# An encoder's RWKV-7 recurrence: each chunk's triangular inverse built as a matrix of its own from powers in 64x64 tiles

## The reference

```python
def _rwkv7_step(S, inp):
    r, w, k, v, a, b = inp
    Sa = jnp.einsum('zbhvk,zbhk->zbhv', S, a)
    S = S * w[..., None, :] + Sa[..., :, None] * b[..., None, :] + v[..., :, None] * k[..., None, :]
    return S, jnp.einsum('zbhvk,zbhk->zbhv', S, r)
```

## Time and profile before

| | |
|---|---|
| time, median of 3 runs | 2095.07 us (2093.65 to 2096.19) |
| profiled execution, its own time | 2095.07 us |
| its span | 2093.1 us |
| TensorE busy | 1840.8 us (88%) |
| VectorE busy | 484.6 us (23%) |
| ScalarE busy | 400.9 us (19%) |
| GpSimd busy | 53.5 us (3%) |
| recurrence, eight pairs | 439.3 to 802.4 us |

### The profile page before, as it was taken

One profiled execution on the slowest core, in us unless ns is written; L12 is line 12 of the kernel. 1 busy time (PEld: TensorE's weight loads), 2 busy tenths in 40 slices (PEclk: granted clock), 3 DMA queues, 4 the chain that ended last, 5 costly groups with the idle time before them and its releaser, 6 DMA issues.

```text
span 2093.1 us, 29565 instructions
## 1 busy us (share of the span) xinstructions
PE 1840.8 (88%) x11998; PEld 1345.0 (64%) x11998; DVE 484.6 (23%) x1116; ACT 400.9 (19%) x1077; POOL 53.5 (3%) x94
## 2 busy tenths in 40 slices
PE   4999999879999999999959988888888998888882
PEld 3788888568889995466647555555645556555451
DVE  1111100677777763010240000000000000000003
ACT  2310000555556551011210000000000000000001
POOL 0000000000000000000000000000000000000000
PEclk9999999979999999999969999999999999999996
DMA  8424653000000007354226999999999999999993
GB/s 286 161 81 161 113 131 141 1 1 1 0 0 0 0 1 274 135 194 161 86 81 256 428 432 418 420 425 434 423 428 420 431 419 425 429 435 428 430 419 159
DMA packets 93162, 505.82 MB, mean 242 GB/s; under 512 B 39076, under 2 KB 43416, under 8 KB 74680
## 3 DMA queue, kind: packets, MB, share of 16 engines
q1 hardware_dynamic: 85456, 487.62, 57.6%
q0 software_dynamic: 6656, 14.12, 1.9%
q10 hardware_dynamic: 1000, 3.37, 0.5%
HBM read 498.76 MB, written 18.91 MB: 247 GB/s over the span
## 4 chain that ended last, share of the span: by engine, by line
PE 69%; DMA 21%; DVE 4%; ACT 3%; issue 2%; SPq 1%; DVEq 0%; ACTq 0%; POOLq 0%
DMA ring<-in_wu 18%; PE ps L1558 16%; PE ps L1211 13%; PE ps L1455 5%; PE ps L1597 5%; PE ps L1548 5%; PE ps L1372 3%; PE ps L1391 3%; PE ps L1473 3%; DMA ring<-in_wd 2%; PE ps L1347 2%; PE ps L1397 1%; PE ps L1514 1%; PE ps L1482 1%; SPq L264 1%
## 5 line engine op out<-in xcount | busy, mean ns | idle before, releaser
L1558 PE MATMUL ps<-ring,rkv 128*64 128x256 f32 x4096 | 484.9, 399 | 73.9 <-DMA ring<-in_wu 42.9
L1558 PEld LDWEIGHTS ps<-ring,rkv 128*64 128x64 f32 x4096 | 335.6, 144 | 232.4 <-DMA ring<-in_wu 51.2
L1211 PE MATMUL ps<-hnT,ring 128*128 128x256 f32 (+1 forms) x1280 | 280.7, 382 | 6.4 <-ACT gg L455 2.2
L1211 PEld LDWEIGHTS ps<-hnT,ring 128*128 128x128 f32 (+1 forms) x1280 | 240.3, 188 | 47.1 <-issue 8.7
L1597 PE MATMUL ps<-ring,gg 128*64 128x512 f32 x1024 | 231.9, 606 | 23.1 <-DMA ring<-in_wd 11.9
L1597 PEld LDWEIGHTS ps<-ring,gg 128*64 128x64 f32 x1024 | 82.3, 139 | 150.6 <-issue 136.6
L1157 DVE SCALAR_TENSOR_TENSOR gg<-ps,tmp,gg 128x256 f32<-128x256 f32 x32 | 15.5, 484 | 532.0 <-PE ps L1558 532.0
L1548 PE MATMUL ps<-hnT,sw 128*128 (+1 forms) x1024 | 120.8, 280 | 7.4 <-DVE hnT L1141 7.4
L1548 PEld LDWEIGHTS ps<-hnT,sw 128*128 128x128 f32 x1024 | 117.8, 195 | 13.3 <-issue 13.3
L1372 PE MATMUL ps<-ring 128*128 128x128 f32 x768 | 114.7, 276 | 0.1
L1372 PEld LDWEIGHTS ps<-ring 128*128 128x128 f32 x768 | 100.3, 192 | 0.8 <-ACT ring L545 0.3
(11 more groups left out here) (315 smaller groups left out, 1719.1 us busy)
## 6 DMA issues: line engine op xcount, KB each, us to landing
ring<-in_wg SPq DMA_DIRECT2D x32, 4096.0 KB, 19.9
ring<-in_wu SPq DMA_DIRECT2D x32, 4096.0 KB, 20.6
ring<-in_wd SPq DMA_DIRECT2D x32, 4096.0 KB, 18.0
ring<-in_w_in SPq DMA_DIRECT2D x7, 4096.0 KB, 14.3
ring<-in_w_out SPq DMA_DIRECT2D x4, 4096.0 KB, 15.8
ring<-in_w_in SPq DMA_DIRECT2D x16, 512.0 KB, 7.5
ring<-in_xatt_wk SPq DMA_DIRECT2D x1, 4096.0 KB, 13.6
ring<-in_xatt_wv SPq DMA_DIRECT2D x1, 4096.0 KB, 13.6
```

The lines of the kernel that those rows point to most:

```text
L1211: ins = mm(ps[0:rows_, t % 4, 0:T], lhs, hnT[:, k, :], start=k == 0, stop=k == KD - 1)
L1558: ins = mm(ps[CAP * h:CAP * h + CAP, bank, 0:T], xT[:, k, CAP * i:CAP * i + CAP], slot_k(slot)[:, k, T * h:T * h + T], start=k == 0, stop= ...
```

## The change

The inverse is no longer applied to X level by level. It is built as a matrix R of its own, and X is multiplied by it once, at the end.

- R begins as I + A, which GpSimd writes for each direction (two additions of 64 partitions x 256 columns each). At each level the square of the power and the power's product with R come out of one set of products, with the same weights, `PN`. GpSimd adds the product to R in levels 1 to 4; VectorE does the last addition, after level 5 (L1014 in the new numbering).
- The products use only the blocks on the diagonal: weights of 64x64 at partitions 0 to 63 and 64 to 127, the output in the same partitions. A group's four products at a level write 64 columns each in levels 0 and 5 and 128 in levels 1 to 4. All four write bank `2 * g`.
- The power and R lie packed in `PR`, 448 columns a group; ScalarE copies 192 (level 0) or 320 columns from PSUM. TensorE turns the power after each of levels 0 to 4 (five times; four before). The turned power is copied to `PN` by ScalarE for groups 0 and 2 and by VectorE for groups 1 and 3.
- The turned old keys (`BKh`) are made after the levels (four pairs of transposes, copied by ScalarE), where before they stood ahead of them.
- VectorE's loop has 10 steps, one for each of its copies to `PN`, and the elementwise work stands behind other steps. Moved to ScalarE: `keys`, and the scaling in `scaled_keys`. Moved to GpSimd: `before` (QA and Q1) and the product in `scaled_keys`.
- ScalarE's square roots stand after level 2, the first half of the exponentials after level 4 and ahead of the old keys, the second half after X's copy.
- TensorE's eight pairs are written out; there is no loop.

The tiles:

```diff
-        PT = W[:, 9216:10240].rearrange("p (g e n) -> p g e n", g=4, e=2)
-        PN = W[:, 10240:11264].rearrange("p (g e n) -> p g e n", g=4, e=2)
+        PR = W[:, 9216:11008].rearrange("p (g n) -> p g n", g=4)
+        R = PR[:, :, 5 * CH:7 * CH].rearrange("p g (e n) -> p g e n", e=2)
+        PN = W[:, 1024:2048].rearrange("p (g e n) -> p g e n", g=4, e=2)
...
+        def two_blocks(x, c, first, second):
+            return x[CH * c:CH * c + CH].rearrange("p (s n) -> p s n", n=CH)[:, first:second + 1:second - first, :]
...
```

GpSimd, in each pair:

```diff
+                    pool.wait_ge(S["rw_about"], p + 1)
+                    pool.tensor_tensor(ew[:, QA], ew[:, Q0], sw[:, 0, ds(p + 1, 1), :].rearrange("p o t -> p (o t)"), ALU.subtract)
+                    pool.tensor_tensor(ew[:, Q1], sw[:, 1, ds(p + 1, 1), :].rearrange("p o t -> p (o t)"), ew[:, CS1],
+                                       ALU.subtract).then_inc(S["rw_q"], 1)
+                for z in range(2):
+                    pool.wait_ge(S["rw_mask"], 4 * p + 2 * z + 2)
...
+                    for c in range(2):
+                        q = slice(CH * c, CH * c + CH)
+                        one = ident[q, q].unsqueeze(1).unsqueeze(1).broadcast_to([CH, 2, 2, CH])
+                        ins = pool.tensor_tensor(R[q, 2 * z:2 * z + 2], GB[q, 2 * z:2 * z + 2, :, 0, q], one, ALU.add)
+                    ins.then_inc(S["rw_r1"], 1)
+                for l in range(1, 5):
+                    for g in range(4):
...
+                        pool.wait_ge(S["rw_pte"], 20 * p + 4 * l + g + 1)
+                        pool.tensor_tensor(PR[:, g, 5 * CH:], PR[:, g, 5 * CH:], PR[:, g, 3 * CH:5 * CH], ALU.add).then_inc(S["rw_ra"], 1)
+                    if l == 2 and not last:
+                        scaled_keys(p)
...
```

ScalarE, in each pair:

```diff
                 for l in range(5):
+                    for g in range(4):
+                        powers(l, g)
+                    for g in (0, 2):
+                        turned_powers(l, g)
...
+                    if l == 2 and not first:
                         head_std(p - 1)
+                    if l == 2 and not last:
                         key_norm(p + 1)
+                if not last:
+                    exponentials(p + 1, 0)
+                for g in range(4):
+                    old_keys(g)
+                for g in range(4):
+                    act.wait_ge(S["rw_xx"], 4 * p + g + 1)
+                    A(X[:, g].rearrange("p m e n -> p (m e n)"), ps[:, 2 * g, 0:T], ACT.Copy).then_inc(S["rw_xe"], 1)
+                if not last:
+                    exponentials(p + 1, 1)
```

VectorE, in each pair:

```diff
-                for step in range(24):
-                    g = step % 4
-                    dve.wait_ge(S["rw_xm"], 24 * p + step + 1)
...
-                    V.tensor_tensor(xf, xf, ps[:, 2 * g, 0:T], ALU.add).then_inc(S["rw_xa"], 1)
+                for step in range(10):
+                    l, g = step // 2, 1 + 2 * (step % 2)
+                    dve.wait_ge(S["rw_tr"], 20 * p + 4 * l + g + 1)
...
+                    V.tensor_copy(PN[:, g].rearrange("p e n -> p (e n)"), ps[:, 2 * g + 1, T:2 * T]).then_inc(S["rw_pnv"], 1)
...
+                for g in range(4):
+                    dve.wait_ge(S["rw_xm"], 4 * p + g + 1)
+                    V.tensor_tensor(PR[:, g, 5 * CH:], PR[:, g, 5 * CH:], ps[:, 2 * g, 3 * CH:5 * CH], ALU.add).then_inc(S["rw_xa"], 1)
```

TensorE, the levels, the product of R and X, and the pairs:

```diff
                         for e in range(2):
-                            o = ps[:, 2 * g, 0:T].rearrange("p (m e n) -> p m e n", m=2, e=2)[:, :, e, :]
-                            ins = mm(o, power(e), X[:, g, :, e, :], start=True, stop=True)
...
-                            for e in range(2):
-                                ins = mm(ps[:, 2 * g + 1, P * e:P * e + P], PN[:, g, e, :], power(e), start=True, stop=True)
-                            ins.then_inc(S["rw_pt"], 1)
+                            for c in range(2):
+                                q = slice(CH * c, CH * c + CH)
+                                if l == 0:
+                                    o, rhs = ps[q, 2 * g, CH * (e + c):CH * (e + c) + CH], GB[q, g, e, 0, q]
+                                elif l < 5:
+                                    o, rhs = two_blocks(ps[:, 2 * g, :], c, e + c, 3 + e), two_blocks(PR[:, g, :], c, e + c, 5 + e)
+                                else:
+                                    o, rhs = ps[q, 2 * g, CH * (3 + e):CH * (4 + e)], R[q, g, e, :]
+                                ins = mm(o, PN[q, g, e, q], rhs, start=True, stop=True)
...
+                for g in range(4):
+                    pe.wait_ge(S["rw_x0ev"], 4 * p + g + 1)
+                    pe.wait_ge(S["rw_xa"], 4 * p + g + 1)
+                    for e in range(2):
+                        for c in range(2):
+                            q = slice(CH * c, CH * c + CH)
+                            o = ps[q, 2 * g, 0:T].rearrange("p (m e n) -> p m e n", m=2, e=2)[:, :, e, :]
+                            ins = mm(o, R[q, g, e, :], X[q, g, :, e, :], start=True, stop=True)
+                    ins.then_inc(S["rw_xx"], 1)
...
-            pair_(0, True, False)
-            with pe.Fori(0, CT - 2) as i:
-                pair_(i + 1, False, False)
-            pair_(CT - 1, False, True)
+            for p in range(CT):
+                pair_(p, p == 0, p == CT - 1)
```

More of the change, by code:

```diff
@@ new lines, in scaled_keys @@
+            def scaled_keys(p):
+                pool.wait_ge(S["rw_kd0"], p + 1)
+                for z in range(2):
+                    ins = pool.tensor_tensor(ew[:, KD0 + z], ew[:, KD0 + z],
+                                             rkv[:, ds(p + 9, 1), :].rearrange("p o t -> p (o t)"), ALU.mult)
+                ins.then_inc(S["rw_kd1"], 1)
+            with pool.Fori(0, CT - 1) as i:
+                pair_(i, False)
+            pair_(CT - 1, True)
+            pool.wait_ge(S["rw_xa"], 4 * CT)
@@ L551, in pair_ @@
-                    if l == 4 and not last:
-                        for half in range(2):
-                            exponentials(p + 1, half)
-                    if l < 4:
-                        for g in range(4):
-                            act.wait_ge(S["rw_tr"], 16 * p + 4 * l + g + 1)
-                            A(PN[:, g].rearrange("p e n -> p (e n)"), ps[:, 2 * g + 1, T:2 * T], ACT.Copy).then_inc(S["rw_pne"], 1)
-                    if l == 1 and not first:
+                        powers(l, g)
@@ L559, in pair_ @@
+                    for g in (0, 2):
+                        turned_powers(l, g)
+                    if l == 0 and not last:
+                        for z in range(2):
+                            ins = A(ew[:, KD0 + z], aa[:, z, ds(p + 1, 1), :].rearrange("p o t -> p (o t)"), ACT.Identity,
+                                    scale=prm[:, ds(p + (P_KA + 1), 1)], bias=dprm[:, ds(p + 31, 1)])
+                        ins.then_inc(S["rw_kd0"], 1)
+                    if l == 2 and not first:
                         head_std(p - 1)
-                    if l == 1 and not last:
+                    if l == 2 and not last:
@@ L905, in pair_ @@
                 if not last:
-                    keys(p + 1)
                     for z in range(2):
@@ L916, in pair_ @@
                         deviation(p - 1, free)
-                    if step == 4 and not first:
+                    if step == 1 and not last:
+                        square_sums(free)
+                    if step == 2 and not first:
                         variance(free)
-                    if step == 5 and not last:
-                        square_sums(free)
-                    if step == 20 and not last:
+                    if step == 9 and not last:
                         bonus(p + 1, free)
-                    xf = X[:, g].rearrange("p m e n -> p (m e n)")
@@ L954, in pair_ @@
+                if not last:
+                    products_bk(p + 1, 0)
                 for g in range(4):
@@ L1377, in pair_ @@
-                        if (l, g) == (1, 0) and not first:
-                            pe.wait_ge(S["rw_dsq"], p)
-                            ins = mm(free, ones2, DSQ, start=True, stop=True)
-                        if (l, g) == (1, 1) and not last:
-                            pe.wait_ge(S["rw_sq"], p + 2)
-                            ins = mm(free, ones2, ew[:, SQ], start=True, stop=True)
-                        if (l, g) == (5, 0) and not last:
-                            pe.wait_ge(S["rw_bonus_in"], p + 2)
-                            ins = mm(free, ones2, ew[:, BON], start=True, stop=True)
@@ L1386, in pair_ @@
[L1386 to L1393 removed]
+                            pe.wait_ge(S["rw_pnv"] if g % 2 else S["rw_pne"], 10 * p + 2 * (l - 1) + g // 2 + 1)
@@ L1394, in pair_ @@
+                        ins.then_inc(S["rw_pt"] if l < 5 else S["rw_xm"], 1)
+                    if l < 5:
                         for g in range(4):
                             pe.wait_ge(S["rw_pte"], 20 * p + 4 * l + g + 1)
+                            free = ps[:, 2 * g + 1, 0:T]
```

(12 more changed lines are left out.)

117 lines of the change are left out of this document (63 added, 54 removed).

## The result

| | before | after |
|---|---|---|
| median | 2094.36 us (2092.67 to 2096.19, 4 runs) | 2135.77 us (2134.42 to 2138.65, 4 runs) |
| profiled execution, its span | 2095.07, 2093.1 us | 2134.42, 2132.6 us |
| recurrence, first Gram product to the last pair's end | 439.27 to 802.41: 363.14 us | 438.10 to 841.04: 402.94 us |
| a middle pair | 45.06 to 45.43 us | 49.95 to 53.36 us |

The changed kernel is slower: ratio 1.0199, 95% interval 1.0182 to 1.0217. The forecast was 2115 us with a range to 2133: the side was right, the size half of what came, and the time lies above the range. All of it is in the recurrence (39.8 us longer in the trace; the span 39.5).

The account below looks back on a forecast made before the run. TensorE was taken to bound the recurrence (44.07 of 45.25 us busy a pair). Later start 4.0 less 0.55 won back gives 3.45 us a pair, +19.6 in all on 2095.07: 2115 us, 8-in-10 range 2088 to 2133.

Parts of the forecast that it names:

- level 1 starts: Level 1 waits for GpSimd's additions for R and starts at 11.7 us of the pair, against 12.46 before.
- wait in level 3, group 3: TensorE waits 2.65 us for VectorE's copy of group 3, behind table load, root and reciprocal.
- wait in level 5: TensorE waits 2.3 us for VectorE's last group 3 copy, behind `products_ar` waiting for exponentials; level ends at 33.4.
- counterpart of L1404 (L1484): Starts at 36.65 us of the pair against 32.67, after old keys' transposes and R times X: 4.0 us later.
- the walk: One steady pair followed step by step through TensorE and the engines it waits for: 3.45 us a pair slower.
- That rival's 2165: Diagonal tiles don't run side by side: groups cost 0.9 instead of 0.45, about +9 a pair, 2165 us; chance 0.08.
- 19.6: Slowdown of the whole kernel in us: six middle pairs 20.7, first pair about +0.5, last about -1.6.
- the switches of shape: TensorE's changes of tile shape, 14 in a pair before L1404's counterpart, cost 0.17 us each.
- the faster rival: Free shape switches (2.4 us a pair), cheaper GpSimd additions (level 1 up to 1.7 earlier): both 2084 us; chance 0.16.
- A lower clock is no case of its own: TensorE's clock stays at 1.00, as in 380 to 390, where it pauses in every step; no cost counted.
- About 0.28 apart: At the pair's end, spacing in us of ScalarE's eight copies of old keys, from 33.95 on, before X's first copy.
- 8.6 + 4 x 0.74 = 11.7 with hand-overs: GpSimd's start: after VectorE's 8.6 us, QA, Q1 and two additions at 0.74 each make R for direction 0.

Follow-up runs that it names:

- e9: The kernel before with TensorE's eight pairs written out, nothing else: 2094.81 us, ratio 1.0003.
- e2 to e4: The changed kernel with one move each: R's additions first on GpSimd; VectorE's waiting instructions behind group 3's copies; old keys early: 2109.28, 2112.20, 2122.10 us.
- e6: The changed kernel with logarithm and exponential on ScalarE in place of roots, reciprocals and their table loads: 2102.36 us, ratio 1.0039.
- e1: The changed kernel with 50 useless transposes a pair in TensorE's three long waits: 2124.03 us, ratio 1.0151.
- e7: The changed kernel with R first, keys early, logarithm and exponential for roots, VectorE's work reordered behind its copies: 2043.09 us, ratio 0.9760.
- e5: The changed kernel with R first on GpSimd, VectorE's waiting instructions behind group 3's copies and old keys early, all together: 2084.63 us, ratio 0.9955.

## Why the prediction was half right

Step by step, from the pair's first product (measured: the pair at full clock):

| step | forecast | measured |
|---|---|---|
| level 1 starts | 11.7 | 12.18 |
| level 2, level 3 start | 15.85, 18.9 | 16.24, 19.20 |
| wait in level 3, group 3 | 2.65 | 2.59 |
| level 4 starts; its waits | 24.6; 0.4 and 1.2 | 24.92; 0.28 and 0.85 |
| wait in level 5; its end | 2.3; 33.4 | 2.38; 33.9 |
| counterpart of L1404 (L1484) | 36.65 | 38.08 |
| its four groups | 3.15 | 3.15 |
| the rest of the pair | 8.9 | 8.72 |
| pair | 48.7 | 49.95 |

The rest is 0.2 us shorter because the loop is gone, as in e9.

**Right.** TensorE's products became too short to cover the other engines, and the waits came where the walk had them, on the engines that it named. The prices held: 0.45 us for a group of 64x64 tiles, 0.73 us for GpSimd's 256 columns, 0.27 instead of 0.30 for level 0. e2 to e4 and e6 show that each of these waits is a cause. The rivals fell. Tiles pair: sixteen products in 1.94 us, both tiles in one bank. By the Trainium skill ("TensorEngine Tiling (Array Packing)", Restrictions and Gotchas) different row tiles can't access the same PSUM bank at once; for diagonal tiles this trace shows otherwise. (That rival's 2165 was also too high by its own terms: 19.6 and, in eight pairs, half of 11 us give 2159.) And the switches of shape cost 0.12 us each instead of 0.17: level 2 lasts 2.96 us (659.33 to 662.29), 0.25 more than 1.8 + 0.91. That goes the faster rival's way, and is too little for it. TensorE's busy share of the recurrence was forecast at about 85%; it is 82%, with the low clock in it.

**Wrong, the larger part: "A lower clock is no case of its own".** It gave a reason, the attention window at clock 1.00 with TensorE pausing in every step. But TensorE was busy 8.93 of 10 us there, and its pauses were short ones:

```profile
384.34 0.66 PE L1299 MATMUL ps<-cst_sb,tmp 128*128 128x128 f32 x4 [0.34 <-ACT tmp L487]
...
387.04 0.66 PE L1299 MATMUL ps<-cst_sb,tmp 128*128 128x128 f32 x4 [0.20 <-ACT tmp L487]
```

The pauses that the forecast itself had worked out, 2.65 us in level 3 and 2.3 us in level 5, had no counterpart there, so the row could not clear them. The one ahead of level 1 the walk had at 0.8 us or more (11.7 - 10.9); it is 2.41 us. e1 puts the price at 11.6 us. With it the first pair is 2.8 us longer than before (forecast 0.5) and the last 1.0 us longer (forecast 1.6 shorter); without it, in e1, they are 1.3 longer and 1.45 shorter.

**Wrong, two terms mis-sized.** "About 0.28 apart" for the copies of old keys, from L557's four in 1.21 us: these copies, of 64 partitions each and in turn of one half and of the other, came 0.39 us apart (3.15 us for eight), 0.9 us a pair. And GpSimd's start: "8.6 + 4 x 0.74 = 11.7 with hand-overs" left 0.14 us for all hand-overs, and level 1 started 0.5 us later. QA began 0.26 us after VectorE's last signal, and Q1 (L365) took 0.91 instead of 0.73 us beside VectorE's L944, which had begun 0.15 us before it:

```profile
652.49 0.48 DVE L944 TENSOR_TENSOR tmp<-tmp 128x256 f32<-128x256 f32 x1
```

In the first pair, which has no such instruction of VectorE there, Q1 took 0.71 us. In e7 the same two meet with Q1 (L379) ahead, and VectorE's (L948) is the long one; alone, in the last pair, it takes 0.43 us:

```profile
564.96 0.73 POOL L379 TENSOR_TENSOR tokA<-sw,tokA 128x256 f32<-128x256 f32 x1
```

```profile
565.06 0.91 DVE L948 TENSOR_TENSOR tmp<-tmp 128x256 f32<-128x256 f32 x1
```

The Trainium skill says that GpSimd shares its SBUF interfaces with VectorE's instructions that have two SBUF inputs ("GPSIMD Engine Reference", section 1). The traces agree: one of the two pays, in these rows the one that starts second.

**The sum.** Forecast 19.6. At full clock (e1) the recurrence is 391.30 - 363.14 = 28.2 us longer: 4.7 us in each of six middle pairs instead of 3.45, and 0.9 us more than forecast in the first and last pair together. The clock adds 11.6: 39.8, as the trace has it. The medians are 41.4 apart; the profiled execution was the fastest of its four.

## What to carry to other kernels

When a change shortens the bounding engine's work, walk the other engines' chain through the same stretch: each instruction that waits for a third engine must stand behind, never ahead of, a copy that the bounding engine needs. When such a walk gives TensorE pauses as long as these (2.4 to 2.6 us), count a lower clock as a case with its own price, and test for it by filling the pauses with useless work. A loss made of waits is no verdict on the idea: the same products, in another order, were faster than the kernel before (e5, 0.45%).

## What the runs showed of the hardware

- Useless work can pay: 50 transposes a pair, 0.11 us each, in TensorE's waits made the kernel 11.7 us faster, since the granted clock stayed at 1.00.
- The same pauses lower the clock in one pair and not in the next (0.87, 0.93, 1.00 with identical instructions); what decides it stays open. A single clean pair of a trace proves nothing about the others.
- ScalarE's copies of 64 partitions x 256 came 0.39 us apart in a row of eight that alternate between halves; those of 128 partitions x 256 took 0.30 each (L626, four in 1.21 us). Alone either takes 0.38 us. No run shows whether the height or the change of halves makes the difference.
- GpSimd's addition and VectorE's instruction with two SBUF inputs, side by side: 0.91 us for the one that started second, where alone they took 0.73 and 0.43 us.
- GpSimd's addition: 0.73 us for 256 columns of 128 or of 64 partitions, 0.43 to 0.55 for 128 columns, by the groups of four in e7's levels (1.70 to 2.21 us).
